# Normed tokens in rows of 2304 bytes, tables moved to make room, and sixteen tokens' mean square taken earlier

## The reference

```python
# first block
h = ada_norm(x, norm1_g, sh1, sc1)               # RMS norm, scaled and shifted by modulation
proj = h @ w_in                                  # 1024 -> 2048 (mixers) + 4096 (gates)
merged = sum(sigmoid(gates_b) * (y_b @ w_branch[b]))   # pool, fourier, hyena, neighbourhood attention
x = x + g1 * (merged @ w_out)
x = x + g2 * conv_ffn(ada_norm(x, norm2_g, sh2, sc2))  # 1024 -> 2 x 2816, conv, silu, -> 1024
x = rmsnorm(x, final_norm_g)
# second block: 16 meta tokens are put ahead of the 512
h = concat(meta, x)
h = h + fox(rms_norm(h, attn_norm))              # 16 heads, causal, with decays; q, k, v, gate, forget
h = h + swiglu(rms_norm(h, ffn_norm))            # 1024 -> 2 x 2816 -> 1024
return rms_norm(h, final_norm)[16:]
```

## Time and profile before

| | us |
|---|---|
| median of 3 runs | 1780.77 |
| lowest and highest | 1779.26, 1781.22 |
| the profiled execution | 1786.97 |
| its span, first to last instruction | 1784.9 |
| PE busy | 1701.3 (95%) |
| DVE, ACT, POOL busy | 916.8, 615.4, 96.1 |

### The profile page before, as it was taken

One profiled execution on the slowest core, in us unless ns is written; L12 is line 12 of the kernel. 1 busy time (PEld: TensorE's weight loads), 2 busy tenths in 40 slices (PEclk: granted clock), 3 DMA queues, 4 the chain that ended last, 5 costly groups with the idle time before them and its releaser, 6 DMA issues.

```text
span 1784.9 us, 20376 instructions
## 1 busy us (share of the span) xinstructions
PE 1701.3 (95%) x8091; PEld 1372.5 (77%) x8091; DVE 916.8 (51%) x1273; ACT 615.4 (34%) x798; POOL 96.1 (5%) x134
## 2 busy tenths in 40 slices
PE   8989979999998899999989999998998999999997
PEld 3468867788886778888878889977886878888886
DVE  4655576566666454444444474234655544444333
ACT  2332348322322243333323443233653332222221
POOL 0100000101110000000000100002431000000000
PEclk9899978999998899999999999999999999999998
DMA  9322101545553223333233322222111333332331
GB/s 322 102 79 78 48 24 48 165 142 167 189 165 118 71 79 96 96 96 89 70 97 112 101 76 69 71 77 69 37 37 44 99 88 95 96 96 69 97 98 47
DMA packets 213924, 170.28 MB, mean 95 GB/s; under 512 B 5444, under 2 KB 202948, under 8 KB 213830
## 3 DMA queue, kind: packets, MB, share of 16 engines
q1 hardware_dynamic: 207222, 144.80, 27.3%
q0 software_dynamic: 6608, 24.19, 4.0%
HBM read 166.84 MB, written 2.13 MB: 95 GB/s over the span
## 4 chain that ended last, share of the span: by engine, by line
PE 87%; DVE 8%; ACT 3%; issue 1%; DMA 0%; DVEq 0%; SPq 0%; ACTq 0%
PE PS L430 23%; PE PS L431 23%; PE PS L432 23%; PE PS L2064 2%; PE PS L439 1%; PE PS L554 1%; DVE WL L91 1%; DVE T L91 1%; PE PS L448 1%; PE PS L449 1%; PE PS L450 1%; PE PS L2049 1%; ACT WH L87 1%; PE PS L589 1%; PE PS L933 1%
## 5 line engine op out<-in xcount | busy, mean ns | idle before, releaser
L430 PE MATMUL PS<-XH,WH 128*128 128x512 f32 (+1 forms) x1280 | 491.5, 384 | 6.3 <-DVE WL L91 5.2
L431 PE MATMUL PS<-XL,WH 128*128 128x512 f32 (+1 forms) x1280 | 491.4, 384 | 0.0
L432 PE MATMUL PS<-XH,WL 128*128 128x512 f32 (+1 forms) x1280 | 489.6, 383 | 0.0
L91 DVE TENSOR_TENSOR WL<-WS,WH 128x2048 fp32r<-128x2048 f32 (+1 forms) x129 | 272.4, 2112 | 250.6 <-ACT WH L87 249.1
L430 PEld LDWEIGHTS PS<-XH,WH 128*128 128x128 f32 x1280 | 240.3, 188 | 60.3 <-DVE WL L91 5.6
L432 PEld LDWEIGHTS PS<-XH,WL 128*128 128x128 f32 x1280 | 240.2, 188 | 49.3
L431 PEld LDWEIGHTS PS<-XL,WH 128*128 128x128 f32 x1280 | 239.9, 187 | 49.4
L87 ACT ACTIVATE WH<-WS 128x2048 fp32r<-128x2048 f32 (+1 forms) x129 | 228.6, 1772 | 73.2 <-PE PS L432 48.6
L430 PE MATMUL PS<-HH,WH 128*128 128x512 f32 x352 | 137.9, 392 | 4.8 <-DVE WL L91 4.8
L431 PE MATMUL PS<-HL,WH 128*128 128x512 f32 x352 | 137.6, 391 | 0.0
L432 PE MATMUL PS<-HH,WL 128*128 128x512 f32 x352 | 137.4, 390 | 0.0
(11 more groups left out here) (357 smaller groups left out, 2405.7 us busy)
## 6 DMA issues: line engine op xcount, KB each, us to landing
WS<-in_w_in SPq DMA_DIRECT2D x24, 1024.0 KB, 5.2
WS<-in_ffn_w_up SPq DMA_DIRECT2D x44, 512.0 KB, 5.1
WS<-in_ffn_w_in SPq DMA_DIRECT2D x44, 512.0 KB, 5.1
MSRC<-in_w_mod POOLq DMA_DIRECT2D x32, 512.0 KB, 4.7
WS<-in_fox_w_in SPq DMA_DIRECT2D x16, 1024.0 KB, 5.6
WS<-in_ffn_w_down SPq DMA_DIRECT2D x16, 704.0 KB, 4.6
WS<-in_ffn_w_out SPq DMA_DIRECT2D x16, 704.0 KB, 4.8
MODW<-in_w_mod SPq DMA_DIRECT2D x8, 1024.0 KB, 11.1
```

Of the source, the lines that this page charges most:

```text
L91: self.e.tensor_tensor(o, a, b, op).then_inc(*self.done.to(*key))
L430: e.matmul(o, lh, rh, start=first and i == 0, stop=False)
L431: e.matmul(o, lh, rl, start=False, stop=False)
L432: ins = e.matmul(o, ll, rh, start=False, stop=last and i == n - 1)
```

## The change

1. XH, XL and SQ get rows of ROW = 576 elements (2304 bytes). The 512 tokens always lie in the last 512 elements, from byte 256 of a row (XHT, XLT, SQT), in both blocks. The 16 meta tokens lie right before them, from byte 192, and the views XH, XL, SQ are the last 528 elements.
2. To make room, the tables below FIX move closer together (FIX 6400 becomes 5632; SM shrinks from 256 to 144 columns). CC, META and MRMS go into the unused heads of the rows of XL and XH, PW and MACC into RST. FB moves into the zone, NCK0 into the room and, for head 0 alone, to NCKF, which lies on KLZ[1]; one of POOL's memsets of KLZ[1] moves behind the second shift for it. PW's transfer moves behind a wait on POOL's queue, and CC is written in eight pieces per partition.
3. The meta tokens' squares become one ScalarE instruction behind the first group's gates (dd = 0), with three adds on VectorE in the second group, the sums matmul inside the last group (i = 22), and the root on ScalarE behind the last group's sigmoids (dd = 3). In out1 the diagonal is first on VectorE's list and only the spread is left on PE behind the first chunk.

```diff
+ROW = 576
-    ID = sbt("ID", [128, 128], F32, 1024 + 128)
-    ONE = sbt("ONE", [128, 128], F32, 1664)
+    ID = sbt("ID", [128, 128], F32, 960)
+    ONE = sbt("ONE", [128, 128], F32, 1472)
...
-    RST = sbt("RST", [128, 528], F32, 4224)
-    FIX = 6400
+    RST = sbt("RST", [128, 528], F32, 3520)
+    FIX = 5632
...
-    XH = sbt("XH", [128, 8, NT], F32R, XO)
-    XL = sbt("XL", [128, 8, NT], F32R, XO + 16896)
-    SQ = sbt("SQ", [128, 8, NT], F32, XO + 16896)
-    ZO = XO + 33792
+    XHR = sbt("XH", [128, 8, ROW], F32R, XO)
+    XLR = sbt("XL", [128, 8, ROW], F32R, XO + 32 * ROW)
+    SQR = sbt("SQ", [128, 8, ROW], F32, XO + 32 * ROW)
+    XH, XL, SQ = (t[:, :, ROW - NT:ROW] for t in (XHR, XLR, SQR))
+    XHT, XLT, SQT = (t[:, :, ROW - L:ROW] for t in (XHR, XLR, SQR))
+    ZO = XO + 64 * ROW
...
-    def terms(w, wl, c, n=128, tok=(0, L), XX=(XH, XL), nk=8, k0=0):
+    def terms(w, wl, c, n=128, tok=(0, L), XX=(XHT, XLT), nk=8, k0=0):
...
-            tm = [terms(w, wl, 128 * m, tok=(c0, c0 + L)) for m in range(2)]
+            tm = [terms(w, wl, 128 * m, tok=(0, L)) for m in range(2)]
...
# gate_pe
+                        if i == 22:
+                            e.wait_ge(*dve.at("meta", "sum"))
+                            e.matmul(bank(7, 1, p1=16, off=8), T[2][:, 0:16], ONE[:, 0:1], start=True,
+                                     stop=True).then_inc(*pe.to("meta", "sums"))
# gate_act
+            if dd == 0:
+                e.wait_ge(*landed("meta"))
+                a.act(T[2][:, 0:128].rearrange("p (k n) -> p k n", k=8), META[:, :, :], ACT.Square, key=("meta", "square"))
+            if dd == 3:
+                e.wait_ge(*dve.at("mod", 22))
+                a.act(ST[0:16, 0:1], bank(7, 1, p1=16, off=8), ACT.Sqrt, bias=SM[0:16, EPSC:EPSC + 1], scale=1.0 / D,
+                      key=("meta", "root"))
             hi_chunk(a, GATE + 5 * dd + 5)
# gate_dve
+            if dd == 1:
+                e.wait_ge(*acts.at("meta", "square"))
+                for w in (64, 32, 16):
+                    v.tt(T[2][:, 0:w], T[2][:, 0:w], T[2][:, w:2 * w], ALU.add, key=("meta", "sum"))
# out1_pe
             if i == 0:
-                mean_pe(e, "meta", 16, MSQ)
+                spread_pe(e, "meta", 16)
# out1_act
-        a.e.wait_ge(*landed("meta"))
-        for k in range(8):
-            square_act(a, "meta", k, META[:, k, :], 16, MSQ)
...
-            if i == 0:
-                root_act(a, "meta", 16)
# out1_dve
-        for k in range(8):
-            square_dve(v, "meta", k, 16, MSQ)
+        diagonal_dve(v, "meta", 16, before="normc")
```

More of the change, by code:

```diff
@@ L247, in build @@
     MGL = zone("MGL", [128, 8, L], F32R, 32)
-    META = sbt("META", [128, 8, 16], F32, ZO + 110 * U8 + 256)
-    MSQ = [sbt(f"MSQ{i}", [128, 16], F32, ZO + 112 * U8 + 64 * i) for i in range(3)]
-    MRMS = sbt("MRMS", [128, 16], F32, ZO + 112 * U8 + 192)
+    META = sbt("METAR", [128, 8, ROW], F32, XO)[:, :, 0:16]
+    MRMS = SQR[:, 0, 0:16]
     QT = zone("QT", [128, 8, L], F32, 0)
@@ L673, in norm1_rest_dve @@
         v.e.wait_ge(*acts.at("norm1", "hi", k))
-        v.tt(XL[:, k, 0:L], SQ[:, k, 0:L], XH[:, k, 0:L].bitcast(F32), ALU.subtract, key=("norm1", "lo", k))
+        v.tt(XLT[:, k, 0:L], SQT[:, k, 0:L], XHT[:, k, 0:L].bitcast(F32), ALU.subtract, key=("norm1", "lo", k))
     def front_dve(v):
@@ L691, in front_dve @@
         for k in range(8):
-            v.tt(SQ[:, k, 0:L], xk(k), bank(3), ALU.mult, key=("norm1", "rooted", k))
+            v.tt(SQT[:, k, 0:L], xk(k), bank(3), ALU.mult, key=("norm1", "rooted", k))
         mod_rows_dve(v, 3)
@@ L741, in front_act @@
         for k in range(8):
-            normed_act(a, "norm1", k, SQ[:, k, 0:L], XH[:, k, 0:L])
+            normed_act(a, "norm1", k, SQT[:, k, 0:L], XHT[:, k, 0:L])
             if k in (2, 5):
@@ L977, in four_pe @@
             for fb in range(2):
-                ins = e.matmul(bank(FOUR_C[tb], 256, off=256 * fb), FU[:, fb, part(tb % 2, tb // 2)], CC[:, :],
+                ins = e.matmul(bank(FOUR_C[tb], 256, off=256 * fb).rearrange("p (k n) -> p k n", k=8),
+                               FU[:, fb, part(tb % 2, tb // 2)], CC,
                                start=True, stop=True)
@@ L1412, in out1_act @@
                 square_act(a, "norm2", n, xk(n))
-            if i == 0:
-                root_act(a, "meta", 16)
         root_act(a, "norm2", L)
         for k in range(8):
-            normed_act(a, "norm2", k, SQ[:, k, 0:L], XH[:, k, 0:L], modcol(3, k))
+            normed_act(a, "norm2", k, SQT[:, k, 0:L], XHT[:, k, 0:L], modcol(3, k))
     def out1_dve(v):
@@ L1433, in out1_dve @@
             if i == 0:
-                diagonal_dve(v, "meta", 16, before="normc")
                 e.wait_ge(*pe.at("meta", "spread"))
-                v.cp(MRMS[:, :], bank(3, 16), key=("meta_rms",))
+                v.cp(MRMS, bank(3, 16), key=("meta_rms",))
             if i == 1:
@@ L1449, in up_bank, with up_pe @@
         return bank(URING[n % 6])
-    def up_pe(e, s, j0, norm, c0, conv):
+    def up_pe(e, s, j0, norm, conv):
         for f in range(22):
@@ L1566, in gained_act @@
         a.e.wait_ge(*dve.at(name, "gained", k))
-        a.act(XH[:, k, 16:NT], SQ[:, k, 16:NT], ACT.Copy, key=(name, "hi", k))
+        a.act(XHT[:, k, 0:L], SQT[:, k, 0:L], ACT.Copy, key=(name, "hi", k))
     def gained_dve(v, name, k, gain):
-        v.ts(SQ[:, k, 16:NT], xk(k), gain, None, ALU.mult, key=(name, "gained", k))
+        v.ts(SQT[:, k, 0:L], xk(k), gain, None, ALU.mult, key=(name, "gained", k))
         v.e.wait_ge(*acts.at(name, "hi", k))
-        v.tt(XL[:, k, 16:NT], SQ[:, k, 16:NT], XH[:, k, 16:NT].bitcast(F32), ALU.subtract, key=(name, "lo", k))
+        v.tt(XLT[:, k, 0:L], SQT[:, k, 0:L], XHT[:, k, 0:L].bitcast(F32), ALU.subtract, key=(name, "lo", k))
     def down1_act(a):
@@ L1715, in foxp_pe @@
                 m = 2 * i + x
-                tm = terms(w, wl, 128 * x, tok=(16, NT))
+                tm = terms(w, wl, 128 * x, tok=(0, L))
                 if m == 0:
-                    prod_by_rows(e, [bank(QB[0]), bank(QB[1])], [terms(w, wl, 128 * y, tok=(16, NT)) for y in range(2)],
+                    prod_by_rows(e, [bank(QB[0]), bank(QB[1])], [terms(w, wl, 128 * y, tok=(0, L)) for y in range(2)],
                                  lambda k: dve.at("norm3", "lo", k), ("q", 1))
@@ L1747, in foxp_pe @@
                     e.wait_ge(*dve.at("k_rooted", m - 2))
-                prod(e, PS[:, 512 * b + HALF0:512 * b + 512], terms(w, wl, 128 * x, tok=(0, NT // 2)))
-                prod(e, bank(b + 1, NT // 2), terms(w, wl, 128 * x, tok=(NT // 2, NT)), ("k", m))
+                prod(e, PS[:, 512 * b + HALF0:512 * b + 512], terms(w, wl, 128 * x, tok=(0, NT // 2), XX=(XH, XL)))
+                prod(e, bank(b + 1, NT // 2), terms(w, wl, 128 * x, tok=(NT // 2, NT), XX=(XH, XL)), ("k", m))
                 if m == 0:
@@ L1789, in foxp_pe @@
         e.wait_ge(*dve.at("k_normed", 7))
-        prod(e, PS[0:16, 512 * 4 + HALF0:512 * 5], terms(w, wl, 0, n=16, tok=(0, NT // 2)))
-        prod(e, bank(5, NT // 2, p1=16), terms(w, wl, 0, n=16, tok=(NT // 2, NT)), ("forget",))
+        prod(e, PS[0:16, 512 * 4 + HALF0:512 * 5], terms(w, wl, 0, n=16, tok=(0, NT // 2), XX=(XH, XL)))
+        prod(e, bank(5, NT // 2, p1=16), terms(w, wl, 0, n=16, tok=(NT // 2, NT), XX=(XH, XL)), ("forget",))
         pe.name("w", j)
@@ L1804, in foxp_pe @@
                     e.wait_ge(*dve.at("decays_turned"))
-                prod(e, bank(m % 4), terms(w, wl, 128 * x, tok=(16, NT)), ("fg", m))
+                prod(e, bank(m % 4), terms(w, wl, 128 * x, tok=(0, L)), ("fg", m))
             if i == 1:
@@ L1971, in build, with decay_tile @@
     ROWOFF = [0, 144, 512, 1008]
+    def decay_tile(h):
+        return NCK[h % 4] if h else NCKF
     def fx_decay_load(e, h):
@@ L2192, in fox_pool @@
                 for i in range(2):
-                    g.memset(z[i][64 - 64 * x:128 - 64 * x, x, :].bitcast(F32), 0.0, key=("fx_zero",))
+                    if (z, i, x) != (KLZ, 1, 0):
+                        g.memset(z[i][64 - 64 * x:128 - 64 * x, x, :].bitcast(F32), 0.0, key=("fx_zero",))
         fx_split_pool(g, 0)
@@ L2200, in fox_pool @@
         fx_shift_pool(g, 1)
+        g.memset(KLZ[1][64:128, 0, :].bitcast(F32), 0.0)
         for i in range(2):
@@ L2262, in tensor @@
         out1_pe(e)
-        up_pe(e, "up1", UP1, "norm2", 0, True)
+        up_pe(e, "up1", UP1, "norm2", True)
         down_pe(e, "down1", "up1", DN1)
@@ L2324, in gpsimd @@
         e.dma_start(CLS[:, :, :], A["four_l"].rearrange("(k p) n -> p k n", p=128)).then_inc(landing("four_l"), 16)
-        e.dma_start(CC[:, :], A["four_c"]).then_inc(landing("four_c"), 16)
+        e.dma_start(CC, A["four_c"].rearrange("p (k n) -> p k n", k=8)).then_inc(landing("four_c"), 16)
+        e.wait_ge(*dve.at("normc", "lo", 7))
+        e.wait_ge(*pe.at("norm1", "spread"))
         e.dma_start(PW[:, :, :], A["pool_wd"]).then_inc(landing("pool_wd"), 16)
```

(1 more changed line is left out.)

47 lines of the change are left out of this document (24 added, 23 removed).

## The result

The changed kernel takes 1762.27 us (median of 5 runs, 1760.39 to 1769.2) against 1781.22 (5 runs, 1779.26 to 1781.68) for the kernel before: 19 us less. The ratio, taken over all the runs, is 0.9907, 95% interval 0.9883 to 0.9931; that is 16.6 us less, and the interval runs from 12 to 21. The prediction was 1758.9, range 1753.0 to 1770.5.

The account below looks back on a forecast made before the run. The prediction took the pace of TensorE's matmul stream, and its few stops, as the bound. Gains of 16.8 and 5.1 us, 21.9 together, off the median 1780.77 gave 1758.9 us, range 1753 to 1770.5.

Parts of the forecast that it names:

- Streaming: 512-column XH and XL matmuls: 5.0 ns less each once all rows start on 256-byte multiples, 16.8 us in all.
- rivals A: XH matmuls: row alignment doesn't matter, HH is faster for another reason; only 5.1 us come, 1775.7 us; chance 7%.
- B: XH matmuls: an aligned row takes 230 ns, gaining 1.7 ns per matmul; 1770.1 us; chance 8%.
- the sum: XH matmul stream: 17.0 us from plain products plus 0.5 us from products taken row by row, before losses at waits.
- gains given back: Three waits for WL behind VectorE: the 48 matmuls before each lose their gain again, 0.7 us.
- The grid: Moving rows starting a multiple of 256 bytes from their tile's start take 226.67 ns, any others 233.3 ns.
- Rival C: HH, YH, MGH, QO: exact multiple of 2048 bytes from WH makes reads collide, so slower; 16 ns each gives 1785; chance 4%.
- The mean square: Sixteen tokens' root moved from out1 to the gate stage: 6.6 us gained, 1.5 us lost, net 5.1 us.
- out1's first chunk: Stall behind this chunk goes: 4.65 us saved, plus 1.9 us from full clock afterwards, together 6.6 us.
- Rival D: Out1 stall filled by another wait, WL of chunk 1 or bank 7 late: 6.6 us vanish; 1765.5 us; chance 6%.
- The price before out1: Gate stage: root and table load delay WH, WL and PE's start of out1; 1.5 us lost, bounds 0 and 1.6.
- The rest: Re-homed tables, CC in eight pieces, PW's wait, moved memset of KLZ[1]: taken as 0, 1.5 us either way.

Follow-up runs that it names:

- the second experiment: Kernel after with the sixteen tokens' root moved behind the high half of out1's first chunk on ScalarE: 1760.17 us, ratio 0.9885.

## Why the prediction was right, and where it was off

**Streaming, right in mechanism and pace, 16.8 us too high by about 1.8.** The pace came down by the predicted 5.0 ns (231.7 to 226.6), without a short k; rivals A (all rows alike) and B (230 ns) are out. Alone, the layout gave 15.0 us; its interval, 12.6 to 17.3, would allow the 16.8, so the time by itself does not show a shortfall. Two traces of the first set do: the kernel with the meta part alone and the unaltered kernel after, on the same chip, whose matmuls stand within 0.1 us of each other up to 89 us. Matched start by start, the last matmuls are 15.4 us apart (1766.70 and 1751.34). Between neighbouring 512-column matmuls at full clock the stream gained 17.3 us, for which the sum had 17.5, and where the starts lie over 0.46 us apart, at waits above all, 1.9 us were lost. The term that was too small is that for gains given back: 0.7 us at three waits for WL. The waits for WL in front of XH grew by 0.9 us from the one kernel to the other (6.0 to 6.9; 5.2 in the kernel before and 6.2 with the layout alone), and the rest went at other stops. That is one execution of each kernel. The moved weights give the same picture from the other side. With the weights 64 bytes up, 5040 matmuls lose 6.67 ns each, 33.6 us; the time rose by 1791.2 - 1762 = 29 (87%). With WL alone, 5040 x 4.44 = 22.4 us; it rose by 18 (80%).

**The grid, right as a rule and wrong as an address.** I put the grid at "a multiple of 256 bytes from the tile's start". XH's tile and the weights stood a multiple of 256 apart, so the rows could not tell the start of the tile from the distance to WH. It is the distance. Rival C took exactly this distance for its subject, but with the opposite sign: an exact multiple is the good case, not the collision. The argument against it, that k = 0 and k = 4 are alike, was true, but the earlier trace rows has one short k only and cannot show it. The whole window from 640 to 860 us of that trace does: from start to start one k takes 690 ns for k = 0 and for k = 4, as means of 40 each, and 695 to 698 for the others.

**The mean square, net 5.1 forecast, 4.6 measured** (by the interval of the ratio 2.9 to 6.4). At out1's first chunk the forecast was 6.6: the gap fell by 4.78 us and full clock behind it gave 1.68 more (chunk 1 starts 15.83 us earlier in the trace of after, the first up stage 17.51), so 6.5. Rival D, another wait in its place, did not come: the WL of chunk 1 starts at 551.80 and is there 6.9 us before PE asks. The price before out1 was forecast at 1.5 us and is 2.0: WL is 1.62 us later against the sigmoid, and VectorE then stands idle for 0.46 us before its sixth branch step, at 540.89. The same 0.46 us stand there in the other traces with the moved mean square, also with the root behind WH (at 547.11), and in neither trace with it in out1. So it came with the move and not with the root; why, I did not find. It is about what the second experiment did not get back (4.42 us of idle time against 4.05). The load ends at 530.67 + 1.28 = 531.95 and the root starts at 531.97. The Trainium skill, "ScalarE: Activation LUTs", section "What ACT_TABLE_LOAD costs", would have a drain of about 1.38 us here; the trace of after disagrees, as that of before did. The measured 4.6 us alone would not tell the forecast 5.1 from the 3.7 that the drain would have left.

**The rest, taken at 0 with 1.5 either way.** Starts of the same matmul show one step against the change, 1.3 us between the start of the second attention (1224.37 and 1200.75) and out2 (1356.98 and 1334.69). About 1.0 of it goes in the first 10 us behind PE's stop of 3.60 us at that start, where the granted clock was 0.64 before (1224.4 to 1234) and 0.52 after (1200.8 to 1211). The moved memset has idle time behind it. No experiment isolates this term; one execution of each kernel is thin for it.

Together: 15.0 + 4.6 = 19.6 instead of 21.9, which is the greater part of the 3.4 us between 1758.9 and 1762.27. The medians of the same runs, 16.3 + 5.3, would leave almost nothing to explain in the parts, so the size of each miss is uncertain by a microsecond or two. The whole change is worth less than 21.9 by both comparisons (intervals 12 to 21 and 16.6 to 21.0).

## What to carry to other kernels

When two groups of matmuls have the same shape and clock but not the same pace, count them over long windows and compare the byte offsets of their operands, moving rows against weights, before anything else: here 64 bytes were 3% of the stream. Keep moving rows and both weight tiles multiples of 256 bytes apart and test the weights' place too, since a grid seen from the moving side alone can belong to the pair. And when an activation that needs another table is put into a gap, put it behind the work for which another engine waits, not merely into a queue that looks idle on average.

## What the runs showed of the hardware

- A 128x512 matmul of these high and low parts, with 128x128 weights, took 226.7 ns at full clock with moving row and weights a multiple of 256 bytes apart, and 233.3 ns at 32, 64 or 128 bytes less (232.3 in the second up stage with 128). Shifting the whole memory image by 128 bytes changed neither pace (840 matmuls in 190 us, as before the shift).
- At 64 bytes more it took 228.9 ns as a mean in most stages, and 233.3 in two stretches of two kernels, with tiles and distances that had 228.9 in the other kernel. What sets it is open; it held from one stop of PE to a later one, so the moment at which the stream starts again is a candidate that no run tested.
- One weight tile of two 64 bytes off cost 231.1 ns, twice what a third of the matmuls would.
- The same products at the front ran at a granted clock of 0.55 in the profiled execution of before and 1.00 in that of after; two spans compared without it would credit 7 us to the change.
